# Selected-keys attention with the logits on key partitions

## The reference, cut to what matters

```python
def dsa_attention(q, k, v, qi, ki, wi):
    ...
        score = jnp.where(causal[None], score, -jnp.inf)
        _, sel = lax.top_k(score, topk)
        k_sel = gather(k, sel)
        v_sel = gather(v, sel)
        logits = jnp.einsum('bqgrd,bqkgd->bqgrk', qg, k_sel).astype(jnp.float32) * att_scale
        valid = sel <= qpos[None, :, None]
        logits = jnp.where(valid[:, :, None, None, :], logits, -jnp.inf)
        p = jax.nn.softmax(logits, axis=-1).astype(v.dtype)
        o = jnp.einsum('bqgrk,bqkgd->bqgrd', p, v_sel)
```

## Time and profile before

| what | value |
|---|---|
| median of 3 runs | 3177.89 us (3175.38 to 3183.56) |
| the profiled execution | 3180.83 us, its span 3179.0 us |
| busy share of the span | PE 93%, PE weight loads 75%, DVE 53%, POOL 37%, ACT 24% |
| granted PE clock, mean | 0.957 |
| attention stage, PE's first to last product | 742.6 to 908.3 us |

### The profile page before, as it was taken

How to read it: one execution, slowest core, us unless ns; L and a number is a source line. 1 busy time by engine, 2 the same in 40 slices (tenths; PEclk the granted TensorE clock), 3 DMA queues, 4 the chain that set the end, 5 groups by cost and what they waited for, 6 DMA issues and landing times.

```text
span 3179.0 us, 35178 instructions
## 1 busy us (share of the span) xinstructions
PE 2945.3 (93%) x13338; PEld 2381.2 (75%) x13338; DVE 1697.7 (53%) x2259; ACT 755.1 (24%) x1320; POOL 1168.0 (37%) x649
## 2 busy tenths in 40 slices
PE   5977999998999899999999779999888999999996
PEld 3765878885778688888888567887676888888885
DVE  4475899985562533232332547888937333333327
ACT  3154000003531211011111245666613000000002
POOL 2320334441024233433444414555532443334331
PEclk9978999996999899999999889999988999999998
DMA  3110112221031011111112110000020111111111
GB/s 136 40 34 14 47 65 81 79 79 66 1 135 71 29 51 47 47 53 46 46 47 66 53 67 27 21 27 27 21 80 27 53 47 48 51 46 46 53 46 60
DMA packets 42300, 165.39 MB, mean 52 GB/s; under 512 B 4688, under 2 KB 5968, under 8 KB 40656
## 3 DMA queue, kind: packets, MB, share of 16 engines
q1 hardware_dynamic: 35568, 129.31, 12.1%
q10 hardware_dynamic: 6624, 34.61, 2.8%
HBM read 147.12 MB, written 16.78 MB: 52 GB/s over the span
## 4 chain that ended last, share of the span: by engine, by line
PE 81%; DVE 10%; issue 5%; ACT 2%; POOL 1%; DVEq 1%; DMA 1%; ACTq 0%; SPq 0%; POOLq 0%
PE dense L457 22%; PE dense L458 21%; PE dense L461 21%; DVE stay L1654 2%; PE dense L799 2%; PE side L708 2%; PE dense L800 2%; PE dense L801 2%; PE dense L718 1%; PE dense L635 1%; PE side L837 1%; DVE a_lo L1319 1%; DVE T L1263 1%; ACT T L977 1%; PE side L497 1%
## 5 line engine op out<-in xcount | busy, mean ns | idle before, releaser
L366 POOL TENSOR_TENSOR w_hi<-raw,zero 128x1024 fp32r<-128x1024 f32 x210 | 404.6, 1926 | 1586.7 <-PE dense L461 1475.4
L457 PE MATMUL dense<-a_hi,w_hi 128*128 128x512 f32 x2192 | 864.9, 395 | 42.4 <-DVE a_lo L1319 20.0
L458 PE MATMUL dense<-a_lo,w_hi 128*128 128x512 f32 x2192 | 860.7, 393 | 0.0
L461 PE MATMUL dense<-a_hi,w_lo 128*128 128x512 f32 x2192 | 681.1, 392 | 0.0
L368 POOL TENSOR_TENSOR w_lo<-raw,w_hi 128x1024 fp32r<-128x1024 f32 x210 | 530.6, 2527 | 16.5
L457 PEld LDWEIGHTS dense<-a_hi,w_hi 128*128 128x128 f32 x2192 | 416.2, 190 | 140.2 <-issue 40.2
L458 PEld LDWEIGHTS dense<-a_lo,w_hi 128*128 128x128 f32 x2192 | 416.1, 190 | 87.6 <-issue 1.2
L461 PEld LDWEIGHTS dense<-a_hi,w_lo 128*128 128x128 f32 x2192 | 415.6, 190 | 87.9
L457 PE MATMUL dense<-b_hi,w_hi 128*128 128x512 f32 x864 | 338.8, 392 | 5.4 <-DVE T L1567 2.5
L458 PE MATMUL dense<-b_lo,w_hi 128*128 128x512 f32 x864 | 336.3, 389 | 0.0
L1547 DVE TENSOR_TENSOR x_res<-x_res,dense 128x1024 f32<-128x1024 f32 x104 | 126.9, 1220 | 332.8 <-PE dense L461 331.1
(11 more groups left out here) (241 smaller groups left out, 3933.0 us busy)
## 6 DMA issues: line engine op xcount, KB each, us to landing
raw<-in_w_stream SPq DMA_DIRECT2D x231, 512.0 KB, 3.4
x_in<-in_x_t SPq DMA_DIRECT2D x4, 1024.0 KB, 8.7
spill_gate<-T ACTq DMA_DIRECT2D x8, 512.0 KB, 2.7
spill_part<-gates ACTq DMA_DIRECT2D x8, 512.0 KB, 2.6
back<-spill_gate ACTq DMA_DIRECT2D x8, 512.0 KB, 3.7
back<-spill_part ACTq DMA_DIRECT2D x8, 512.0 KB, 4.7
x_res<-in_x_t ACTq DMA_DIRECT2D x2, 2048.0 KB, 8.6
spill_x<-x_res ACTq DMA_DIRECT2D x1, 4096.0 KB, 12.6
```

Of the source, the lines that this page charges most:

```text
L366: pool.tensor_tensor(w_hi[:, r % 2, :], raw[:, r, :], zero[:, 0:1].broadcast_to([P, D]), ALU.add).then_inc(weights_rounded, 1)
L457: pe.matmul(o, w_hi[:, slot, w], hi[:, k, x], start=b == 0, stop=False)
L458: pe.matmul(o, w_hi[:, slot, w], lo[:, k, x], start=False, stop=False)
L461: last = pe.matmul(o, w_lo[:, slot, w], hi[:, k, x], start=False, stop=stop)
```

## The change

The stage is written anew with keys on partitions. A step is now a query block i and a group g (16 steps, s), and within it one block of 128 keys (72 in all, x), with the group's three heads side by side as 384 columns.

- Operands: `k_stack` holds the keys' hi part in 64 rows and their lo part in the other 64, and `v_ones` holds a group's values beside 64 columns of ones (ACT and DVE make both before the convolution tiles). `qd_hi` and `qd_lo` hold the queries' two parts doubled over both halves of the rows, made per step by ACT (`round_queries`) and DVE (`split_queries`), two instructions of 64x384 each.
- First pass, per step and head: PE computes logits with queries on partitions from the hi part of the queries (`bound_logits`, float32r, 128 rows); DVE adds the mask and takes the maximum (`bound`). Per step DVE negates three of them, PE turns the three columns into one row of 384 (`turn_bounds`, three fp32 products with the identity), ACT copies that row (`copy_bounds`).
- Second pass, per key block: four float32r products into one bank (keys by `qd_hi`, keys by `qd_lo`, mask by three identities, ones by the row of bounds); ACT takes exp of 128x384; PE multiplies `v_ones` by it in fp32, so that 64 of the 128 result rows are the sum of the weights. No transposes and no copies of them.
- Per step DVE inverts the 64x384 sums and multiplies.
- The mask is made by POOL in six instructions after the meet, the first two blocks' by DVE much earlier. The barrier no longer waits for line 1476. `m_in` is loaded after the stage. Some buffers move (`ya_hi`, `ya_lo`, `back`).

```diff
-DSA_PLAN = [(i, h) for i in range(TB) for h in range(ATT_H)]
+DSA_PLAN = [(i, g) for i in range(TB) for g in range(GROUPS)]
+DSA_KEYS = [(s, kb) for s, (i, g) in enumerate(DSA_PLAN) for kb in range(i + 1)]
+DSA_X0 = [DSA_KEYS.index((s, 0)) for s in range(DSA_STEPS)] + [len(DSA_KEYS)]
+DSA_LEAD, DSA_LAG = 3, 2
...
+            pool.wait_ge(picked, 1)
+            for i in range(TOPK // P, TB):
+                sc = slice(score_at(i), score_at(i + 1))
+                pool.tensor_scalar(mask_r[:, sc], score[:, sc], TAKEN / 2, NEG, ALU.is_gt, ALU.mult).then_inc(masked, 1)
...
+            def bound_logits(n):
+                s, j = n // REP, n % REP
+                i, g = DSA_PLAN[s]
+                pe.wait_ge(dup_split, s + 1)
+                if n >= 2:
+                    pe.wait_ge(d_max, n - 1)
+                if n >= REP + 1 and j == 1:
+                    pe.wait_ge(d_rowc, s)
+                for c in range(0, P * (i + 1), 512):
+                    e = min(P * (i + 1), c + 512)
+                    last = pe.matmul(side[:, n % 2, c:e], qd_hi[:, s % 4, j, :], k_stack[:, g, c:e], start=True, stop=True)
+                last.then_inc(d_ready, 1)
+            def turn_bounds(s):
+                pe.wait_ge(d_neg, s + 1)
+                for h in range(REP):
+                    e = REP * (s % 2) + h
+                    last = pe.matmul(bound_bank(s)[:, h * P:h * P + P], neg_max[:, e:e + 1], ident[:, :], start=True,
+                                     stop=True, skip_group_check=True)
+                last.then_inc(d_row, 1)
+            def att_logits(x):
+                s, kb = DSA_KEYS[x]
...
+                if x >= 2:
+                    pe.wait_ge(d_exp, x - 1)
+                o = att_logit_bank(x)
+                pe.matmul(o, k_stack[:, g, keys], qd_hi[:, s % 4, :, :], start=True, stop=False)
+                pe.matmul(o, k_stack[:, g, keys], qd_lo[:, s % 4, :, :], start=False, stop=False)
+                pe.matmul(o, mask_r[:, score_at(i) + kb * P:score_at(i) + kb * P + P], ident3[:, :, :], start=False, stop=False)
+                pe.matmul(o, one_row[:, :], bound_row[:, s % 2, :], start=False, stop=True).then_inc(d_logits, 1)
+            def att_values(x):
+                s, kb = DSA_KEYS[x]
+                if kb == 0 and s >= 2:
+                    pe.wait_ge(d_copied, s - 1)
+                pe.wait_ge(d_exp, x + 1)
+                pe.matmul(att_out_bank(s), v_ones[g][:, kb, :], att_w[:, x % 4, :], start=kb == 0, stop=kb == i
+                          ).then_inc(d_out, 1)
+            for n in range(REP * DSA_LEAD):
+                bound_logits(n)
+                if n % REP == REP - 1:
+                    turn_bounds(n // REP)
+            for x in range(len(DSA_KEYS) + DSA_LAG):
+                if x < len(DSA_KEYS):
+                    att_logits(x)
+                if x + 1 in DSA_X0[DSA_LEAD - 1:DSA_STEPS - 1]:
+                    turn_bounds(DSA_X0.index(x + 1) + 1)
+                for n in BOUND_AT.get(x, ()):
+                    bound_logits(n)
+                if x >= DSA_LAG:
+                    att_values(x - DSA_LAG)
...
+                    act.activation(att_w[:, x % 4, :], att_logit_bank(x), ACT.Exp, scale=SCALE).then_inc(d_exp, 1)
...
-            sc = score[:, score_at(2):score_at(TB)]
-            dve.tensor_scalar(sc, sc, TAKEN / 2, NEG, ALU.is_gt, ALU.mult)
+            dve.drain().then_inc(picked, 1)
             meet(dve, "dve", met_n)
...
+                    dve.wait_ge(d_out, e + 1)
+                    dve.reciprocal(att_inv[:, s % 2, :], att_out_bank(s)[HD:P, :])
+                    dve.drain()
+                    dve.tensor_tensor(ya_f[group_rows(g), :, i * P:i * P + P],
+                                      att_out_bank(s)[0:HD, :].rearrange("p (j q) -> p j q", j=REP),
+                                      att_inv[:, s % 2, :].rearrange("p (j q) -> p j q", j=REP), ALU.mult).then_inc(d_copied, 1)
```

More of the change, by code:

```diff
@@ L697, in _ @@
             meet(pe, "pe", met_n)
[L700 to L712, removed]
-                if n >= 2:
[L714 to L720, removed]
+            pe.wait_ge(kv_split, GROUPS)
@@ L1003, in _ @@
             meet(act, "act", met_n)
+            for g in range(GROUPS):
+                act.activation(k_stack[group_rows(g), g, :], k_f[group_rows(g), :], ACT.Copy).then_inc(kv_round, 1)
+            for g in range(GROUPS):
+                act.activation(v_ones[g][:, :, 0:HD], v_f[:, :, HD * g:HD * g + HD], ACT.Copy)
+                act.activation(v_ones[g][:, :, HD:P], v_f[:, :, HD * g:HD * g + HD], ACT.Copy, bias=1.0, scale=0.0)
             for j in range(3):
@@ L1073, in _, with att_high, round_queries @@
-            meet(act, "act", met_n)
+            def att_high(i):
+                act.wait_ge(d_copied, GROUPS * (i + 1))
+                act.activation(ya_hi[:, :, i * P:i * P + P], ya_f[:, :, i * P:i * P + P], ACT.Copy).then_inc(parts["ya"][0], 1)
+            def round_queries(s):
+                i, g = DSA_PLAN[s]
+                if s >= 4:
+                    act.wait_ge(d_logits, DSA_X0[s - 3])
+                for half in (g, 1 - g):
+                    last = act.activation(qd_hi[group_rows(half), s % 4, :, :], q_f[group_rows(g), :, i * P:i * P + P], ACT.Copy)
+                last.then_inc(dup_round, 1)
@@ new lines, in split_queries, with bound @@
+            def split_queries(s):
+                i, g = DSA_PLAN[s]
+                dve.wait_ge(dup_round, s + 1)
+                for half in (g, 1 - g):
+                    last = dve.tensor_tensor(qd_lo[group_rows(half), s % 4, :, :], q_f[group_rows(g), :, i * P:i * P + P],
+                                             qd_hi[group_rows(g), s % 4, :, :].bitcast(F32), ALU.subtract)
+                last.then_inc(dup_split, 1)
+            def bound(n):
+                s, e = n // REP, REP * (n // REP % 2) + n % REP
+                i = DSA_PLAN[s][0]
+                w = P * (i + 1)
+                dve.wait_ge(d_ready, n + 1)
+                dve.wait_ge(masked, max(0, i - 1) + 1)
+                dve.tensor_tensor_reduce(out=masked_out[:, n % 2, 0:w], in0=side[:, n % 2, 0:w],
+                                         in1=mask_r[:, score_at(i):score_at(i) + w].bitcast(F32), scale=1.0, scalar=TAKEN, op0=ALU.add,
+                                         op1=ALU.max, accum_out=row_max[:, e:e + 1]).then_inc(d_max, 1)
+                if n % REP == REP - 1:
+                    e -= REP - 1
+                    dve.drain()
+                    if s >= 2:
+                        dve.wait_ge(d_row, s - 1)
+                    dve.tensor_scalar(neg_max[:, e:e + REP], row_max[:, e:e + REP], -1.0, None, ALU.mult).then_inc(d_neg, 1)
```

130 lines of the change are left out of this document (92 added, 38 removed).

## The result

The changed kernel takes 3197.14 us (median of 5 runs, 3194.39 to 3198.21) against 3177.89 for the kernel before: a ratio of 1.0058, 95% interval 1.0046 to 1.0070. It is slower by 0.58%. The forecast was 3171, with 3156 to 3192 as its range. The profiled execution took 3197.14 us, its span is 3195.2, its mean clock 0.961.

What follows compares the result with a forecast made beforehand. PE's own work at two clocks was taken to bound the stage; barrier, entry, steps and tail put PE's restart at 904, 6.5 us before 910.5, so 3180.8 became 3174.3, less 2.9 for the median: 3171.4, range 3156 to 3192.

Steps and rivals of the forecast that it cites:

- What bounds the kernel now: Attention stage: PE's own work at two clocks; at most 29 us to gain by the clock, 6 by waits.
- The step that failed: Fourth product of each key block: one row costs as much as 128, four products 0.72 us, block 1.43 us.
- 0.2 more for the group: Old logits products at the full clock: 1.71 us for their columns and 0.2 us more for the group.
- the walk: First six key blocks, steps 0 to 3: 25 us at half clock, 22 with its rise; step 4 at 780.
- Steps 4 to 7: Their 14 key blocks: PE needs 26 us, DVE 29 to 30, so DVE binds narrowly, to 810.
- The barrier: Before the stage: line 1476's hold goes, the meet moves from 742.5 to 740.6; gain 1.9 us.
- The clock: PE's clock in the first six key blocks: rises around 770, to 1.00 between 765 and 775.
- The rival of a low clock to 800: Attention stage: clock rises only at 800, restart at 914, time 3181; range 3176 to 3187, chance 0.20.
- The inverse: DVE's 64x384 inverse per step: 2.6 us with the start, from the slope of 6.25 ns an element.
- DVE under PE's 8.8 to 13 us a step in steps 8 to 15: Last eight steps: DVE needs 8.5 to 9 us a step, so PE binds, 87 us together, ending at 897.
- the rival with DVE and the chains: Inverse 4 us, each chain 1 us more: restart 927, time 3194; chance 0.18 for 3187 up, shared with low clock past 815.
- The tail: Stage's end to PE's restart on the output projection: 5.5 us, before 2.1, with inverse and product between; restart at 904.

Runs made afterwards that it cites:

- e1: Changed kernel with the row of bounds and the ones of the fourth product on 128 rows, zeros added, in place of 1: 3176.26 us.
- e3: Changed kernel with the row of bounds and the ones of the fourth product on 32 rows in place of 1: 3195.36 us.
- e5: e1 with the inverse left out, a copy of the sums in its place: 3160.32 us.
- e6: e1 with the subtraction that makes the queries' low parts of steps 4 to 15 moved from DVE to POOL: 3182.31 us.
- e7: e6 with ACT making diagonals of the negated bounds for the fourth product, without turn products and row copies: 3175.33 us.
- e11: e7 with the queries' low parts made a whole step earlier, in eight slots in place of four: 3146.45 us.
- e10: e1 with turn products and copy given later, and low parts of steps 4 to 15 on POOL a step earlier in eight slots: 3174.44 us.

## Why the prediction was wrong

**What bounds the kernel now: right.** PE's own work set the stage, before and, behind the entry, after.

**The step that failed** is the sentence "The product by one row of ones costs as much as one of 128 rows, since columns are what is paid." It gave 1.43 us a block. Measured: 1.73 with one row, 1.73 with 32 rows, 1.34 with 128 (e1, e3). The four full-height products and the value product would have been 0.09 cheaper than forecast; the short one made them 0.30 dearer. The sign stood in the trace of before and was passed over: the "0.2 more for the group" of the 64-row logits products, which was put down to starting a group, has the same late load: in all 45 places the first load of 64 rows starts together with its product, while loads of 128 rows start ahead of theirs. No run gave that product full height.

**Step by step**, the changed kernel's times with 1.5 us added. First product of the key blocks 759.8, forecast 758. Step 4 at 783.5, forecast 780. Step 8's first block (x=20) at 816.8, forecast 810. End of PE 922.4, forecast 898.5. The increments are +1.8, +1.7, +3.3 and +17.1. The last is 52 blocks x 0.30 = 15.6 and little else; of steps 4 to 7, 14 x 0.30 = 4.2 stands against it. In the first six blocks three things were dearer than counted: at the half clock L788 cost 0.45 and 0.62 us around itself where 0.32 and 0.32 were counted (1.7 in four blocks), the clock rose 3.5 us later in the forecast's times (1.7), and it fell again (1.6). That is 5.0 against the 1.7 measured, so the rest of the walk was some 3 us too dear; that its end came out near is in part luck.

**Steps 4 to 7: the wrong engine.** The forecast had DVE bind there narrowly. PE waited 2.1 of 33.3 us for DVE: at 1.73 us a block PE's own work was the longer.

**The barrier** was right: ACT and DVE pass it 2.9 us after the last spill's issue (736.55 to 739.42), as the transfer's 2.6 us said, and DVE, without line 1476, stands idle for 2.88 us before it. From the last gate addition to the next transfer it is 4.61 us, before 6.23: 1.6 gained, forecast 1.9.

**The clock** rose near 772 (0.51 from 770 to 772, 1.00 from 772 to 774); the forecast said 770. The rival of a low clock to 800 is out. But the low stretches at 778.75 and at the tail, 3.5 us each, weren't in the forecast. With them the clock is low for 41 us in place of 62, and some 10 of the 29 us that it held were taken.

**The inverse**: 2.559 us, forecast 2.6 by the slope of the earlier trace rows. The page "VectorE: DVE Perf Modes" of the Trainium skill (First, the fixed hardware budget) had led to an estimate of 3.2; the trace lies a fifth below.

**DVE under PE's 8.8 to 13 us a step in steps 8 to 15: right for the wrong block.** It held only since the block took 1.73. At 1.34, DVE's work and the chains through it held PE: e5 gained 15.9 us from a cheaper inverse, the clock's part included. So the rival with DVE and the chains gave the right time, 3194, by the wrong mechanism; its inverse of 4 us isn't there.

**The tail**: 5.1 us from PE's last product to its restart, forecast 5.5. What was left out is that PE restarts at 0.50 after 5.05 us of idleness. Its first four products take 0.76 to 0.63 us, before 0.47 to 0.39, and from the restart to DVE's `T<-dense,back` it is 5.9 us, before 4.5: 1.4 us.

**Line 1441's wait** near 411 us (now L1568) is 5.64 us, before 5.65: the added work before the convolution tiles was absorbed, as forecast.

The sum: 1.8 + 1.7 + 3.3 + 17.1 for PE's end, less 0.4 in the tail, and 1.4 for the clock behind it, are 24.9 us. The measured median lies 25.7 above the forecast. Of them 20 are the key blocks of steps 4 to 15, by the one sentence on the row of ones.

## What to carry to other kernels

A product on few rows between products on all rows is not cheap: count its cost by a row of the same neighbourhood, and if its operands can be padded with zeros to full height, do that (here 19 us for no added column). It was dear with 1, 32 and 64 rows beside 128, and not with 96. When the bound moves from one engine to another, move work off the critical engine only together with its lead: moving the low parts to POOL cost some 6 us when they came just in time (e6), and making them a step earlier was worth 29 (e7 to e11). Read the clock of every variant before pricing a wait: PE's waits of 1.4 to 3.9 us were followed by stretches at the half clock in some places, and the waits' own length doesn't show that. And a turned row that shares a bank with the next product of the chain is a place where the order decides.

## What the runs showed of the hardware beyond that

The load for a product on 1 row behind one on 128 starts only with its own product: 0.25 us of idle time before it at the full clock, and 0.18 before the full-height load behind it; 32 rows give the same block time. Loads of 64 rows behind products on 128 start with their product too (before, 883.44). With 128 rows beside 128, or 96 beside 128 (before, 186.62 to 186.92), there is no such idle time. One column of weights on 128 rows (the turn) behind 128 columns starts as late: 0.27 us after the product before it (e10, 852.11).

In the changed kernel TensorE's clock stood at 1.00 from 782.25 us until it waited 5.05 us for the last `ya_lo`, and at 0.50 from 925.5 to 929. After a tail's wait of 2.17 us in the kernel before it stayed at 1.00 (window 910.5 to 912.5), and so it did after 3.05 us in e5. But after 1.97 us at 777.35 it fell to 0.50 for 3.5 us, so the length of the wait alone doesn't decide.

Work on 64x384 elements: the inverse 2.56 us on DVE; a subtraction 0.58 on DVE and 0.99 on POOL. POOL's masks took 16 us in six instructions, 3.6 for 1024 columns, over three times as long as DVE for the same columns (4.49 us for 4224). The forecast had said 4.5 to 9; they were hidden all the same.
